# Projection columns streamed as 280 and 240 tokens, with the 240's high and low parts in one matmul

## The reference

```python
def run_layer(h, p_i, pos0, pool_prefix, attend, lam_init, ...):
    xn = rmsnorm(h, g_mix)
    proj = xn @ w_in                                  # 2048 -> 4096
    q, k, v, u = jnp.split(proj, [1024, 2048, 3072], axis=-1)
    q, k = rope(q), rope(k)
    o = attend(q, k, v, lam)                          # differential softmax, 8 heads
    o = rmsnorm(o, g_sub) * (1.0 - lam_init)
    pool_out, pool_state = pool_mixer(u, pool_prefix, pos0, w_pool, pool_scale)
    h = h + jnp.concatenate([o, pool_out], axis=-1) @ w_out          # 2048 -> 2048
    gate, up = jnp.split(rmsnorm(h, g_ffn) @ w_gate_up, 2, axis=-1)  # 2048 -> 11264
    h = h + (jax.nn.silu(gate) * up) @ w_down                        # 5632 -> 2048
    h = h + jax.nn.sigmoid(rmsnorm(h, g_ple) @ w_ple_gate) * (p_i @ w_ple_proj)
```

## Time and profile before

| | us |
|---|---|
| median of 3 runs | 2316.01 |
| lowest and highest | 2315.81, 2317.71 |
| profiled execution, first to last instruction | 2313.3 |
| TensorE matmuls busy in it | 2261.3 |
| VectorE, ScalarE, GpSimdE busy | 1640.3, 1081.3, 191.3 |

### The profile page before, as it was taken

How to read it: one execution, slowest core, us unless ns; L and a number is a source line. 1 busy time by engine, 2 the same in 40 slices (tenths; PEclk the granted TensorE clock), 3 DMA queues, 4 the chain that set the end, 5 groups by cost and what they waited for, 6 DMA issues and landing times.

```text
span 2313.3 us, 45786 instructions
## 1 busy us (share of the span) xinstructions
PE 2261.3 (98%) x18549; PEld 2212.4 (96%) x18549; DVE 1640.3 (71%) x2131; ACT 1081.3 (47%) x1645; POOL 191.3 (8%) x88
## 2 busy tenths in 40 slices
PE   7999999999999999999999999999999999999997
PEld 7988898888999999999999999999999999989997
DVE  5366555565257888888888888888777778786433
ACT  5334454454245554554445455454444444455334
POOL 0032112301221000000000000000000000121111
PEclk9999999999999999999999999999999999999999
DMA  8455565544335445454554545456967667533332
GB/s 269 128 167 160 180 193 178 170 121 138 88 91 160 131 128 161 141 173 141 158 154 129 159 133 173 141 172 195 302 183 226 193 189 199 143 87 101 88 98 74
DMA packets 484535, 359.51 MB, mean 155 GB/s; under 512 B 8513, under 2 KB 465298, under 8 KB 483513
## 3 DMA queue, kind: packets, MB, share of 16 engines
q1 hardware_dynamic: 473225, 347.31, 50.6%
q10 hardware_dynamic: 11208, 10.78, 1.4%
HBM read 301.23 MB, written 57.29 MB: 155 GB/s over the span
## 4 chain that ended last, share of the span: by engine, by line
PE 93%; DVE 4%; ACT 1%; DMA 1%; issue 1%; SPq 0%; ACTq 0%; DVEq 0%
PE acc L1190 40%; PE acc L749 31%; PE scores L1190 16%; PE scores L749 2%; PE mail_bank L749 1%; PE o_bank L749 1%; DMA x_low<-act_low_rows 1%; DVE w_low L2458 1%; DVE w_low L2017 0%; PE mail_bank L911 0%; DVE key_pages L2462 0%; PE mail_bank L1337 0%; SPq L666 0%; DMA small<-in_lambda_k 0%; DVE small L2141 0%
## 5 line engine op out<-in xcount | busy, mean ns | idle before, releaser
L1190 PE MATMUL acc<-x_high,w_high 128*128 128x260 f32 x1584 | 448.4, 283 | 6.9 <-DVE w_low L2458 4.8
L1190 PE MATMUL acc<-x_low,w_high 128*128 128x260 f32 x1584 | 447.1, 282 | 0.0
L1190 PE MATMUL acc<-x_high,w_low 128*128 128x260 f32 x1584 | 446.8, 282 | 0.0
L749 PE MATMUL acc<-x_high,w_high 128*128 128x260 f32 (+2 forms) x2048 | 436.8, 291 | 5.9 <-DVE w_low L2017 2.9
L749 PE MATMUL acc<-x_high,w_low 128*128 128x260 f32 (+2 forms) x2048 | 421.5, 284 | 0.0
L749 PE MATMUL acc<-x_low,w_high 128*128 128x260 f32 (+2 forms) x2048 | 421.2, 284 | 0.0
L2458 DVE TENSOR_TENSOR w_low<-raw,w_high 128x1024 fp32r<-128x1024 f32 (+4 forms) x252 | 285.5, 1133 | 117.2 <-ACT w_high L1757 116.3
L2458 DVE TENSOR_TENSOR w_low<-key_pages,w_high 128x1024 fp32r<-128x1024 f32 (+4 forms) x252 | 284.3, 1136 | 93.7 <-ACT w_high L1757 93.0
L749 PEld LDWEIGHTS acc<-x_high,w_high 128*128 128x128 f32 x2048 | 319.4, 190 | 28.3 <-issue 21.2
L749 PEld LDWEIGHTS acc<-x_high,w_low 128*128 128x128 f32 x2048 | 320.4, 190 | 0.0
L749 PEld LDWEIGHTS acc<-x_low,w_high 128*128 128x128 f32 x2048 | 320.2, 189 | 0.0
(11 more groups left out here) (318 smaller groups left out, 4012.8 us busy)
## 6 DMA issues: line engine op xcount, KB each, us to landing
raw<-in_w_gate_up SPq DMA_DIRECT2D x44, 1024.0 KB, 6.6
key_pages<-in_w_gate_up SPq DMA_DIRECT2D x44, 1024.0 KB, 7.5
raw<-in_w_in SPq DMA_DIRECT2D x32, 1024.0 KB, 7.1
act_high_rows<-late_rounded SPq DMA_DIRECT2D x22, 910.0 KB, 5.3
act_low_rows<-late_rounded SPq DMA_DIRECT2D x22, 910.0 KB, 6.9
key_pages<-in_cache_k SPq DMA_DIRECT2D x32, 512.0 KB, 5.5
late<-in_cache_v SPq DMA_DIRECT2D x32, 512.0 KB, 5.8
raw<-in_w_out SPq DMA_DIRECT2D x16, 1024.0 KB, 5.9
```

The source lines that it names most:

```text
L749: return pe.matmul(o, l, r, start=start, stop=stop)
L1190: return pe.matmul(bank, w, x, start=start and first, stop=last, skip_group_check=True)
```

## The change

- `x_high` and `x_low` become two halves of one tensor, `x_parts`, so that one access pattern can read the same tokens of both.
- A k step of a plain column (`long_product`) issues five matmuls: high x high and high x low of tokens 0 to 279 (280 columns each) into the end of the accumulator's first bank; high weights on tokens 280 to 519 of both parts (480 columns) into its second bank, side by side; low x high of 280; low x high of 240. The columns streamed are 1560 as before. All 520 sums lie side by side (`tokens_of`), and the high x low sums of the last 240 tokens lie behind them (`late_lows`).
- Those 240 are added when the column is taken. For q and k, ScalarE copies them to SBUF (`copy_lows`), VectorE adds the copy to the accumulator (`add_lows`), and `swap` now waits for that. For v, u and the PLE gate (`scaled`), VectorE also multiplies the 240 by `rstd` into a scratch row, which frees the accumulator, and adds the row. For the output projection VectorE adds the accumulator, waits, and adds the 240; the second add frees it.
- The PLE sigmoid waits for a new semaphore `gated` and not for `acc_free`. The FFN and the two quartered PLE columns are as before.

The diff, cut to its core:

```diff
+TA = 280
+TB = T - TA
+A_AT = 512 - TA
-        xh = sb("x_high", [P, KD, T], F32R)
-        xl = sb("x_low", [P, KD, T], F32R)
+        x_parts = sb("x_parts", [P, 2, KD, T], F32R)
+        xh, xl = x_parts[:, 0], x_parts[:, 1]
...
+        def tokens_of(i):
+            return flat_acc[i][:, A_AT:A_AT + T]
+        def late_lows(i):
+            return acc[i][:, 1, TB:2 * TB]
...
+            def long_product(i, w_high, w_low, k, first, last):
+                early, late_one = acc[i][:, 0, A_AT:512], acc[i][:, 1, 0:TB]
+                late_both = acc[i][:, 1, 0:2 * TB].rearrange("p (a n) -> p a n", a=2)
+                mm(early, w_high, xh[:, k, 0:TA], start=first, stop=False)
+                mm(early, w_high, xl[:, k, 0:TA], start=False, stop=False)
+                mm(late_both, w_high, x_parts[:, :, k, TA:T], start=first, stop=last)
+                mm(early, w_low, xh[:, k, 0:TA], start=False, stop=last)
+                return pe.matmul(late_one, w_low, xh[:, k, TA:T], start=False, stop=last, skip_group_check=True)
...
-                    ins = product(pair, wh[slab.home][:, k * P:(k + 1) * P],
-                                  wl[slab.home][:, k * P:(k + 1) * P],
-                                  xh[:, k, :], xl[:, k, :], k == 0, k == KD - 1)
+                    at = slice(k * P, (k + 1) * P)
+                    ins = long_product(i, wh[slab.home][:, at], wl[slab.home][:, at], k, k == 0, k == KD - 1)
...
+            def copy_lows(n, t):
+                act.wait_ge(S["acc_ready"], t + 1)
+                if n:
+                    act.wait_ge(S["lows_added"], n)
+                act.activation(lows_of(n), late_lows(t % 2), ACT.Copy).then_inc(S["lows_copied"], 1)
             def swap(n, t):
-                act.wait_ge(S["acc_ready"], t + 1)
+                act.wait_ge(S["lows_added"], n + 1)
...
             for h in range(NH):
+                copy_lows(h, h)
                 swap(h, h)
...
+                    elif i == 5:
+                        copy_lows(NH + g + 1, turn(k_slab(g + 1)))
                     elif i == 6:
                         swap_k(g + 1)
...
-                    act.wait_ge(S["acc_free"], PLE_T + m + 1)
+                    act.wait_ge(S["gated"], m + 1)
...
+            def add_lows(n, t):
+                dve.wait_ge(S["lows_copied"], n + 1)
+                late_one = acc[t % 2][:, 1, 0:TB]
+                tt(late_one, late_one, lows_of(n), ALU.add).then_inc(S["lows_added"], 1)
+            def scaled(dest, t, lows):
+                tt(dest, tokens_of(t % 2), rstd[:, :], ALU.mult)
+                V.says(tt(lows, late_lows(t % 2), rstd[:, TA:T], ALU.mult), S["acc_free"], t + 1)
+                V.wait()
+                V.step(tt(dest[:, TA:T], dest[:, TA:T], lows, ALU.add))
+                V.wait()
...
             for h in range(NH):
+                add_lows(h, h)
                 rotate(h, h, q_all[:, h, :])
...
-                V.says(tt(halves(v_now[:, :]), acc[t % 2][:, :, 0:HT], halves(rstd[:, :]), ALU.mult), S["acc_free"], t + 1)
-                V.wait()
+                scaled(v_now[:, :], t, v_nat[:, TB:2 * TB] if h == 0 else lows_dve)
...
                     elif i == 6:
                         dots(g + 1, 2)
+                    elif i == 7:
+                        add_lows(NH + g + 1, turn(k_slab(g + 1)))
...
-                tt(tile, pair[:, :, 0:HT], tile, ALU.add).then_inc(S["acc_free"], 1)
+                V.step(tt(tile, tokens_of(i), tile, ALU.add))
+                V.wait()
+                tt(tile[:, TA:T], late_lows(i), tile[:, TA:T], ALU.add).then_inc(S["acc_free"], 1)
...
-                    V.says(tt(halves(gate_row[s]), acc[s][:, :, 0:HT], halves(rstd[:, :]), ALU.mult), S["acc_free"], t + 1)
+                    tt(gate_row[s], tokens_of(s), rstd[:, :], ALU.mult)
+                    V.says(tt(gate_low, late_lows(s), rstd[:, TA:T], ALU.mult), S["acc_free"], t + 1)
+                    V.wait()
+                    tt(gate_row[s][:, TA:T], gate_row[s][:, TA:T], gate_low, ALU.add).then_inc(S["gated"], 1)
```

More of the change, by code:

```diff
@@ L326, in layer, with lows_of @@
         e_row = late[0:16, 7168:7168 + PAST]
+        lows_dve = late[:, 7680:7680 + TB]
+        def lows_of(n):
+            return v_nat[:, 0:TB] if n <= NH else late[:, 7680 + TB:7680 + 2 * TB]
         state = region[0:NB * PS, 0:PW]
@@ L762, in begin, with part_of @@
                     pe.wait_ge(S["acc_free"], t - 1)
-            def part_of(slab, pair, t, ks, waits=None):
+            def part_of(slab, i, ks, waits=None):
                 for k in ks:
@@ L774, in part_of, with whole @@
                 return ins
-            def whole(slab, pair, t, waits=None, first=False):
-                begin(slab, t, first)
-                part_of(slab, pair, t, range(KD), waits)
+            def whole(slab, i, t):
+                begin(slab, t)
+                part_of(slab, i, range(KD))
             def stats(phase):
@@ L1081, in _, with out_weights @@
                 segment(g, lambda i: dense((u_slab(g), k_slab(g + 1), v_slab(g + 1))[i // 8], i % 8))
+            def out_weights(m, k):
+                slab = Slab(OUT_N + m)
+                return tuple(w[slab.home][:, k * P:(k + 1) * P] for w in (wh, wl))
             def out_first(m, k):
-                slab = Slab(OUT_N + m)
-                w_high, w_low = (w[slab.home][:, k * P:(k + 1) * P] for w in (wh, wl))
+                w_high, w_low = out_weights(m, k)
+                early = acc[m][:, 0, A_AT:512]
@@ L1092, in out_second @@
             def out_second(m, k):
[L1094 to L1098, removed]
-            def out_both(m, k):
[L1102 to L1106, removed]
-                                 start=a == 1 and k == NH and n == 0, stop=k == KD - 1 and n == 2)
-                return ins
+                w_high, w_low = out_weights(m, k)
@@ new lines, in out_second @@
+                late_both = acc[m][:, 1, 0:2 * TB].rearrange("p (a n) -> p a n", a=2)
+                mm(late_both, w_high, x_parts[:, :, k, TA:T], start=False, stop=False)
+                pe.matmul(acc[m][:, 1, 0:TB], w_low, xh[:, k, TA:T], start=False, stop=False, skip_group_check=True)
+            def out_both(m, k):
+                w_high, w_low = out_weights(m, k)
+                early, last = acc[m][:, 0, A_AT:512], k == KD - 1
+                late_both = acc[m][:, 1, 0:2 * TB].rearrange("p (a n) -> p a n", a=2)
+                mm(early, w_high, xh[:, k, 0:TA], start=False, stop=False)
+                mm(early, w_high, xl[:, k, 0:TA], start=False, stop=False)
+                mm(late_both, w_high, x_parts[:, :, k, TA:T], start=k == NH, stop=last)
+                mm(early, w_low, xh[:, k, 0:TA], start=False, stop=last)
+                return pe.matmul(acc[m][:, 1, 0:TB], w_low, xh[:, k, TA:T], start=False, stop=last, skip_group_check=True)
@@ L1530, in swap_k @@
                 swap(NH + h, turn(k_slab(h)))
+            copy_lows(NH, turn(k_slab(0)))
             swap_k(0)
```

68 lines of the change are left out of this document (35 added, 33 removed).

## The result

The changed kernel takes 2337.26 us, median of 4 runs (2336.84 to 2338.58), against 2315.91 for the kernel before beside it: 1.0096 times as long, 95% interval 1.0084 to 1.0108 (the ratios of the experiments below have theirs in brackets too). The forecast was 2314.0 with a range to 2323, so it was wrong by 23 us, in the direction that it had given 22%. Of its parts mostly the signs held: a gain in the matmuls, losses where columns are taken.

What follows compares the result with a forecast made beforehand. TensorE, busy for 98% of the span, was taken as the bound. Matmuls 11.2 us less and column takes 8.35 more, net -2.85, gave 2313.2 from the median 2316.0; it said 2314, range 2306 to 2323.

Steps and rivals of the forecast that it cites:

- Fourth place: Taking v in segments 1, 3, 5, 7: 0.55 us later each, 2.2 in all; 0 to 0.1 each in 2, 4, 6.
- main case: The forecast's own account of gain and losses holds: by itself 2309.5 to 2319 us, chance 0.60.
- The gain: Plain columns: one matmul fewer in each of 992 k steps, 11.5 ns each, 11.2 us less in all.
- the leftover grows with the columns: Rival on matmul cost, supported by plain float32 matmuls' 3 ns leftover: gain only 2.9 us, 2321.5 us, chance 0.14.
- those rivals: Long matmuls cheaper, 2284 or 2306 us, chance 0.08; 240-column matmul at plain float32 price, 2606 us, chance 0.07.
- First q column: VectorE's add delays the swaps, so TensorE begins q column 2 about 2.4 us late, partly at half clock: 1.8 us lost.
- Last q column: TensorE already waits 1.12 us there; copy, add and two hand-overs now come ahead of the swap: 1.0 us lost.
- Segment 0: The k(0) chain is 1.0 us later and taking v adds two instructions: 1.3 us lost, between 0.8 and 1.8.
- Last segment: VectorE also makes the output projection's operands there: 0 to 1.6 us lost, taken as 0.8.
- Into the FFN: VectorE is busy 12.97 of 13 us there; two column takes just ahead add 2 x 0.45: 0.9 us lost.
- PLE: Into the PLE columns: the first column's extra VectorE and ScalarE time delays `w_low`, which TensorE awaits: 0.35 us lost.
- The clock as a rival: New stalls bring one more half-clock stretch near 61 or 740 us, 1.7 us each: 2317 to 2320 us, chance 0.06.

Runs made afterwards that it cites:

- Experiment 2: The kernel after with GpSimd's products made on 8 of their 1024 columns, work left out: 2322.2 us, ratio 1.0030 to the kernel before.
- experiment 4: The kernel before with one added VectorE add of 8 columns, two SBUF operands, between the multiply of v and the copy: 2330.5 us, ratio 1.0066.
- experiment 5: The kernel after with GpSimd's products held back until VectorE has combined the segment's first probabilities, all work done: 2324.7 us, ratio 1.0039.
- experiment 1: The kernel after with v taken by VectorE instructions that read at most one operand from SBUF: 2330.9 us, ratio 1.0066.
- experiment 10: The kernel after with GpSimd's products held back, q columns as before, tokens cut at 264 and 256, long matmul 512 columns: 2317.7 us, ratio 1.0012.
- second profiled execution: The kernel after itself, unchanged, profiled once more; when timed again it took 2337.0 us, ratio 1.0096.

## Why the prediction was wrong

**Fourth place, segments: the step that failed, and the cost of the case.** The prediction priced v's take as added instructions (0.35 + 0.44 us, 0.8 with the hand-overs) and kept the copy at the 0.58 of the earlier trace rows; so v would be 0.3 us late in odd segments and covered by the mixing products in even ones: 1.65 us for segments 1 to 6. They cost 14.8. The two added instructions did take what they were priced at: 0.40 us, and 0.41 for the add where it met no product (0.52 to 0.54 where it did). But the copy's 0.58 was no duration, it was a wait for GpSimd, and shifted by 0.8 us it no longer met the end of a product but the beginning of the next. Experiment 2 takes GpSimd's products away and the cost goes; experiment 4 makes the same shift in the old kernel with one short instruction and the cost comes; 5 moves the products out of the way. The sign stood in the trace of before, in the durations of one line for one shape: 172, 576 and 1625 ns.

The Trainium skill, SBUF — State Buffer, section SBUF: two separate sides, says that VectorE with two SBUF inputs (or a copy in its fast mode) and a GpSimd instruction that reads SBUF want the same pair of ports, that whichever starts first holds it for its whole instruction, and the other fully blocks. The traces agree: 2.20 us for 0.17 beside products of 2.5, and experiment 1, whose multiplies and adds with one operand in PSUM ran in 0.41 to 0.70 us while products ran. This rule spoke against the change and the prediction didn't weigh it.

A smaller slip is in its sums: the bounds of its seven losses add up to 7.05 and 11.65 us, not 6.7 and 12, and with those that it used the main case runs from 2310.7, not 2309.5, to 2319.5. Nothing hangs on it.

**The gain: the size of the term was wrong, by a factor of 4.6 a k step (11.5 ns against 2.5), and of 8 in all (11.2 us against 1.4).** The step "one matmul per k step goes, 11.5 ns each" assumed a leftover that is fixed per matmul, from three sizes within 8 columns of each other, and carried it to 480. The prediction had put its lower bound at 3 ns (2.9 us in all) with the float32 pair as its sign, and gave "the leftover grows with the columns" 0.14. That rival had the size nearly right: its 2.9 us is close to the 2.5 by the k step, and the slope of 0.46 ns a column that the prediction measured gives 119.8 + 220 x 0.46 = 221 ns for 480 columns, measured 219. Its mechanism is not shown. The short matmuls all carry about 12 ns over streaming (112 ns for 240 columns, 120 for 260, 129 on average for 280), and the two long ones 19 ns both (219 for 480, 233 for 512 in experiment 10), so the leftover did not grow from 480 to 512. The long matmuls are also the only ones that read their tokens as two runs, one from each part; whether the 7 ns come from the length or from the second run was not tried. The long matmul was neither cheap nor the 240 one slow (112 ns); those rivals fell. The cited gap of 2.5 ns a matmul comes near the net 2.5, but as the sum of +5.0 and -2.5: no run shows 2.5 ns as the price of a matmul.

**First q column: right in mechanism and place.** TensorE began q column 2 at 58.82, forecast 58.75:

```profile
58.82 1.21 PE L768 MATMUL acc<-x_parts,w_high 128*128 128x280 f32 x3 [2.30 <-DVE region L2137]
```

The clock took the upper case: half until 64, two stretches, so 3.3 us, the forecast's "between 1.8 and 3.5" and not its 1.8. In the second profiled execution the wait was 2.30 us again, one stretch followed, and the column cost 2.4. **Last q column:** the wait is 2.00 us, forecast 2.1, 0.9 more than the earlier trace rows; but behind it came a half-clock stretch of 1.5 us, which made 1.0 into 2.4.

```profile
138.27 1.04 PE L1102 MATMUL scores<-constants,small 128*8 128x128 f32 x8 [2.00 <-DVE small L2157]
```

**Segment 0:** 0.8 for 1.3, within its bounds. There the copy took 0.17, having missed the products by luck, which hid 1.5 us that the old kernel's copy had lost (1.62). **Last segment:** 1.4 for 0.8, but not by its mechanism: the stall of 1.53 us at 553 has the length that it had before (at 532), and the old kernel ran on at full clock behind it, the new one at half. **Into the FFN:** TensorE waits 1.1 us more, as forecast (0.9), and yet the stage came out 0.5 ahead, since the half-clock stretch that the old kernel had at 742 didn't come. **PLE:** 0.15 for 0.35; 0.7 at the last column were in no term.

**The clock as a rival** was given 0.06 and one more stretch. There are three more in net (two in the second profiled execution), and the count moves with every variant. They are some 4 us of the loss, all but one of them behind stalls that the other terms made; the one in the last segment stands behind a stall that the kernel before had too.

## What to carry to other kernels

When one line's durations for one shape differ within a trace (172 to 1625 ns), it may be waiting inside, and then shifting it by a fraction of a microsecond can cost a whole instruction of whoever holds it: look at what GpSimd does beside every VectorE instruction that reads two SBUF operands, and keep such instructions off the path while it works, or hold GpSimd back. A leftover per matmul read from sizes 8 columns apart says nothing on one of twice the size; test the long matmul before multiplying the leftover by a thousand. Price a new stall of about 2 us on TensorE with the 1.4 us of half clock that may follow it.

## What the runs showed of the hardware

- VectorE and GpSimd take turns instruction by instruction: with products of 2.4 to 2.5 us back to back, each VectorE instruction that reads two SBUF operands, or copies within SBUF, waits for the end of one (0.41, then 2.1 us in experiment 4), whatever its own size. A product of GpSimd is stretched in turn: in segments 1 to 6 of the kernel after the first of each group took 3.6 to 4.4 us, with VectorE's `w_low` of two operands (2.29 us) beside it, and in experiment 5, where it ran later, 2.4.
- fp32r matmuls in a stream, k step of 1560 columns: 6 x 260 720.8 ns; 3 x 280 and 3 x 240 723.3; 280, 280, 480, 280, 240 718.3; 264, 264, 512, 264, 256 715.8. Joining two of 240 is worth 5.0 ns. Matmuls of two columns go by at 112 ns from start to start, and so do those of 240, so 240 seem to be just under what the load of weights allows; that this floor is the reason for the 2.5 ns of the uneven cut is an inference from these numbers.
- The half clock came in stretches of 3.4 or 6.8 us in all of these traces, start and tail left out. Of two stalls of the same 1.53 us at the same place of the program (the last segment, before and after), one was followed by it and one was not; of the stalls of 1.87 us at v, those of segments 3 and 5 were and that of segment 1 was not. What decides is left open.
